# GpSimd makes the low part of every fourth weight unit of a float32 decoder layer

## The reference, cut to what matters

```
h = x + 1/2 * SwiGLU_1(norm(x))
z = norm(h) @ W_mix_in          # columns split into B, C, H (conv group), U, V (gMLP group)
h = h + concat(conv part, gated part) @ W_mix_out
h = h + XAttn(norm(h), norm(mem))
h = h + 1/2 * SwiGLU_2(norm(h))
out = norm_final(h)
```

## Time and profile before

| what | us |
|---|---|
| median of three runs | 2155.09 |
| lowest and highest run | 2153.47, 2155.34 |
| the profiled execution, its time | 2154.91 |
| its span, from the first to the last instruction | 2153.2 |
| PE busy | 2139.6 |
| DVE busy | 1388.9 |
| ACT busy | 991.8 |
| POOL busy | 2.3 |

### The profile page before, as it was taken

How to read it: one execution, slowest core, us unless ns; L and a number is a source line. 1 busy time by engine, 2 the same in 40 slices (tenths; PEclk the granted TensorE clock), 3 DMA queues, 4 the chain that set the end, 5 groups by cost and what they waited for, 6 DMA issues and landing times.

```text
span 2153.2 us, 25537 instructions
## 1 busy us (share of the span) xinstructions
PE 2139.6 (99%) x9584; PEld 1776.2 (82%) x9584; DVE 1388.9 (65%) x1611; ACT 991.8 (46%) x1104; POOL 2.3 (0%) x7
## 2 busy tenths in 40 slices
PE   9999999999999999999999999999999999999998
PEld 7888888888888888888888888888888888888886
DVE  5676667666475557868898554576676667764544
ACT  6444444444344444444554444454544444443433
POOL 0000000000000000000000000000000000000000
PEclk9999999999999999999999999999999999999999
DMA  7766666665556566665556555566666666665654
GB/s 232 219 186 199 192 193 193 195 195 191 193 181 206 181 201 184 199 216 184 185 191 201 165 163 174 162 216 195 191 191 195 194 193 188 196 196 194 195 194 139
DMA packets 159489, 412.20 MB, mean 191 GB/s; under 512 B 12604, under 2 KB 14260, under 8 KB 159028
## 3 DMA queue, kind: packets, MB, share of 16 engines
q1 hardware_dynamic: 158000, 410.04, 61.4%
q10 hardware_dynamic: 1412, 1.11, 0.2%
HBM read 409.01 MB, written 2.10 MB: 191 GB/s over the span
## 4 chain that ended last, share of the span: by engine, by line
PE 96%; DVE 2%; ACT 1%; DMA 0%; issue 0%; ACTq 0%; SPq 0%; DVEq 0%
PE ps L990 94%; PE ps L1019 1%; DVE w_lo L606 1%; PE ps L1003 1%; DVE ps L666 1%; PE ps L1068 0%; DVE convT L812 0%; DMA raw<-in_w_ffn_in 0%; ACT w_hi L336 0%; ACT convT L469 0%; PE ps L1134 0%; DVE stage L802 0%; ACTq L409 0%; ACT scratch L586 0%; ACT zT L466 0%
## 5 line engine op out<-in xcount | busy, mean ns | idle before, releaser
L606 DVE TENSOR_TENSOR w_lo<-raw,w_hi 128x1024 fp32r<-128x1024 f32 x768 | 936.2, 1224 | 707.5 <-ACT w_hi L336 700.9
L336 ACT ACTIVATE w_hi<-raw 128x1024 fp32r<-128x1024 f32 x767 | 810.7, 1061 | 1077.3 <-PE ps L990 1046.2
L990 PE MATMUL ps<-w_hi,xT_hi 128*128 128x512 f32 x1848 | 570.1, 390 | 1.6 <-DVE w_lo L606 1.6
L990 PE MATMUL ps<-w_lo,xT_hi 128*128 128x512 f32 x1848 | 569.2, 389 | 0.0
L990 PE MATMUL ps<-w_hi,xT_lo 128*128 128x512 f32 x1848 | 569.2, 389 | 0.0
L990 PEld LDWEIGHTS ps<-w_hi,xT_hi 128*128 128x128 f32 x1848 | 346.4, 188 | 73.8 <-DVE w_lo L606 1.2
L990 PEld LDWEIGHTS ps<-w_hi,xT_lo 128*128 128x128 f32 x1848 | 347.0, 188 | 72.0
L990 PEld LDWEIGHTS ps<-w_lo,xT_hi 128*128 128x128 f32 x1848 | 347.0, 188 | 72.0
L990 PE MATMUL ps<-w_hi,hidT_hi 128*128 128x512 f32 x704 | 218.3, 390 | 0.4 <-DVE w_lo L606 0.4
L990 PE MATMUL ps<-w_lo,hidT_hi 128*128 128x512 f32 x704 | 218.2, 389 | 0.0
L990 PE MATMUL ps<-w_hi,hidT_lo 128*128 128x512 f32 x704 | 218.2, 389 | 0.0
(11 more groups left out here) (126 smaller groups left out, 851.7 us busy)
## 6 DMA issues: line engine op xcount, KB each, us to landing
raw<-in_w_ffn_in SPq DMA_DIRECT2D x352, 512.0 KB, 4.2
raw<-in_w_ffn_out SPq DMA_DIRECT2D x176, 512.0 KB, 4.3
raw<-in_w_mix_in SPq DMA_DIRECT2D x80, 512.0 KB, 4.3
raw<-in_w_mix_out SPq DMA_DIRECT2D x32, 512.0 KB, 4.1
raw<-in_w_xq SPq DMA_DIRECT2D x32, 512.0 KB, 4.3
raw<-in_w_xk SPq DMA_DIRECT2D x32, 512.0 KB, 4.2
raw<-in_w_xv SPq DMA_DIRECT2D x32, 512.0 KB, 3.7
raw<-in_w_xo SPq DMA_DIRECT2D x32, 512.0 KB, 3.7
```

What stands on the lines that cost most here:

```text
L336: nc.scalar.activation(w_hi[:, k % RING, :], raw[:, k % RAW, :], ACT.Copy).then_inc(hi_ready, 1)
L606: nc.vector.tensor_tensor(w_lo[:, k % RING, :], raw[:, k % RAW, :], w_hi[:, k % RING, :].bitcast(F32), ALU.subtract).then_inc(lo_ready, 1)
L990: ins = nc.tensor.matmul(bank(s, t * GW + b * BLK, BLK), xs[:, k, t * P:(t + 1) * P], ws_[:, k % RING, b * BLK:(b + 1) * BLK], start=(k == ...
```

## The change

The low part of slot 3 goes to GpSimd, with a semaphore `lo_pool` of its own. DVE's `lo_units` leaves these units out. PE and SP wait for `lo_pool` or `lo_ready` according to the unit's slot. GpSimd makes the 66 units of the groups before `C`, then the mask of `w_spatial`, then the other 126.

```diff
+def low_parts(unit0, n):
+    base = (unit0.base if isinstance(unit0, Turn) else unit0) + n
+    pool = base % RING == 0
+    count = base // RING if pool else (RING - 1) * (base // RING) + base % RING
+    if isinstance(unit0, Turn):
+        count = unit0.i * (unit0.step // RING * (1 if pool else RING - 1)) + count
+    return pool, count
...
+        lo_pool = sem("lo_pool")
...
+        def wait_low(engine, unit0, n):
+
+            pool_made, count = low_parts(unit0, n)
+            engine.wait_ge(lo_pool if pool_made else lo_ready, count)
...
                     if not (isinstance(unit0, int) and unit0 + k < RAW):
-                        sp.wait_ge(lo_ready, unit0 + (k - RAW + 1))
+                        wait_low(sp, unit0, k - RAW + 1)
...
+            def low(hi_count):
+
+                pool.wait_ge(hi_ready, hi_count)
+                nc.gpsimd.tensor_tensor(w_lo[:, RING - 1, :], raw[:, RAW - 1, :], w_hi[:, RING - 1, :].bitcast(F32),
+                                        ALU.subtract).then_inc(lo_pool, 1)
+
+            units = sum(n for _, n in groups)
+            with pool.Fori(0, UNIT0["C"] // RING) as i:
+                low(i * RING + RING)
             pool.wait_ge(ws_loaded, 16)
             pool.affine_select(out=ws[:, :, :], in_=ws[:, :, :], compare_op=ALU.is_ge, fill=0.0, base=0,
                                pattern=[[0, HEADS], [-1, P]], channel_multiplier=1).then_inc(ws_masked, 1)
+            with pool.Fori(0, (units - UNIT0["C"]) // RING) as i:
+                low(i * RING + (UNIT0["C"] + RING))
...
             def lo_units(unit0, k0, k1):
                 for k in range(k0, k1):
+                    if k % RING == RING - 1:
+                        continue
                     dve.wait_ge(hi_ready, unit0 + (k + 1))
...
                 for k in range(k0, k1):
-                    pe.wait_ge(lo_ready, unit0 + (k + 1))
+                    wait_low(pe, unit0, k + 1)
```

More of the change, by code:

```diff
@@ L48, in starts, with __init__, __add__, __mul__ @@
     return at
+class Turn:
+    def __init__(self, i, base, step):
+        self.i, self.base, self.step = i, base, step
+    def __add__(self, n):
+        return self.i * self.step + (self.base + n)
+    def __mul__(self, n):
+        return self.i * (self.step * n) + self.base * n
+def low_parts(unit0, n):
[5 more added lines that the diff above has]
+    return pool, count
 def build(nc, x, mem, g_ffn1, w_ffn1_in, w_ffn1_out, g_mix, w_mix_in, conv_w, conv_b, g_gm_v, w_spatial, b_spatial,
@@ L271, in load_ffn_in @@
                     for j in range(2):
-                        load_units(ffn_in_src(w, i * GW + (1 + j) * BLK), i * (2 * KD) + (u0 + (1 + j) * KD), KD)
+                        load_units(ffn_in_src(w, i * GW + (1 + j) * BLK), Turn(i, u0 + (1 + j) * KD, 2 * KD), KD)
             def load_pair(name, w, n):
@@ L391, in ffn_in @@
                     for j in range(2):
-                        unit0 = i * (2 * KD) + (u0 + (1 + j) * KD)
+                        unit0 = Turn(i, u0 + (1 + j) * KD, 2 * KD)
                         hi_units(unit0, 0, 4)
-                        silu(j, unit0)
+                        silu(j, unit0 + 0)
                         hi_units(unit0, 4, 11)
```

## The result

| | before | changed |
|---|---|---|
| median of 20 runs, us | 2154.62 | 2157.38 |
| lowest and highest, us | 2152.9, 2155.41 | 2156.17, 2158.59 |
| span of the profiled execution, us | 2153.2 | 2156.2 |
| DVE busy, us | 1388.9 | 1172.5 |
| POOL busy, us | 2.3 | 469.1 |

The ratio is 1.0014, with a 95% interval from 1.0008 to 1.0021: 3.0 us slower (1.7 to 4.5), where 3.7 us was forecast.

What follows compares the result with a forecast made beforehand. TensorE was taken as the bound, with low parts nearly always early. The end 1.2, V 0.65 and U 1.9 us summed to 3.75 us, giving 2158.8 us (+0.17%) from a median of 2155.09, range 2154.8 to 2165.0.

Steps and rivals of the forecast that it cites:

- What bounds the kernel: Whole kernel: TensorE is the bound, busy 2139.6 of 2153.2 us; freeing DVE gains only where PE waits, 2.0 us in all.
- The price: GpSimd's subtraction in slot 3: 2.35 us plus 0.1 us to start, so its low part lands 1.18 us later than DVE's.
- my count by streams: Price of GpSimd's subtraction: three streams against the mask's two, 1.5 x 1.57 us, giving 2.35 us.
- my high end: Price of GpSimd's subtraction if all is done twice: 2 x 1.57 = 3.14 us.
- The two engines hold each other up: A DVE instruction with two SBUF inputs waits until GpSimd's has ended, and the other way round; one row showed 0.57 us.
- The end: Last unit, in slot 3: its low part comes 1.18 us later and counts in full, +1.2 us.
- Group U: Unit 6 of U: GpSimd's unit 7 and DVE's L835 run one after the other, so the low part is late, +1.9 us.
- The start of V: Convolution steps held until GpSimd's unit 15 ends, starting at 858.25 instead of 857.61; +0.65 us.
- ffn1_out1 and xo1: Transposing stretches: nothing, just; DVE held at unit 6 but in time, and unit 13 stays where it was.
- the slow rival: Subtraction near 3.14 us: end 2.0, V 1.45, U 2.7, ffn1_out1 and xo1 3.2 us; sum 9.4, 2164.5 us; chance 0.33.
- The quiet rhythm: Steady units: nothing lost; PE's margin goes from 5.58 to 4.40 us and the two engines hardly meet.
- the bound of 6.8 us: Quiet rhythm: PE would begin to wait only if the subtraction took 1.23 + 5.58 = 6.8 us.

Runs made afterwards that it cites:

- unit 7 of U alone: The kernel before, with the single low part of unit 7 of group U made by GpSimd and the other 767 by VectorE; 2155.59 us, ratio 1.0009.
- the copy: The changed kernel, with GpSimd copying the raw unit to the low part's place instead of subtracting (result altered); 2152.82 us, ratio 0.9993.
- its order changed: The changed kernel, with GpSimd starting unit 7 of U only once VectorE has made the low part of unit 6; 2155.13 us, ratio 1.0008.
- three units of B alone: The kernel before, with only units 3, 7 and 11 of group B made by GpSimd; 2153.78 us, ratio 0.9997.
- last low part in two halves: Changed kernel with units 15 of B, 7 of U and the last given back to VectorE, the last made in two halves; 2151.84 us, ratio 0.9992.
- twofold: The changed kernel, with GpSimd making each of its low parts twice over; 2196.78 us, ratio 1.0198.
- threefold: The changed kernel, with GpSimd making each of its low parts three times over; 2756.32 us, ratio 1.2795.

## Why the prediction came out as it did

The forecast was 2158.8 us, +0.17%; measured were 2157.38 us, +0.14%. The mechanism was right, and so were the two main places and their sizes. The price behind them came out by luck, the term for V was 0.4 us too large, and the nothing for ffn1_out1 and xo1 had a wrong reason. Step by step:

- **What bounds the kernel.** Right. DVE lost 216 us of busy time and TensorE gained nothing from it except at V, where one low part had been late.
- **The price, 2.35 us and 0.1 us to start.** 2.40 and 0.08 us (the high part at the end is over at 2135.63, GpSimd starts at 2135.71). This was luck. The mask's 1.57 us, from which I counted, held waiting already. In the kernel with unit 7 of U alone the same mask runs where no DVE instruction overlaps it:

```profile
55.05 1.09 POOL L379 TENSOR_SCALAR_AFFINE_SELECT ws<-ws 128x1024 f32<-128x1024 f32 x1 [53.51 <-DMA ws<-in_w_spatial]
```

So 0.48 us of 1.57 were waiting, behind the DVE subtraction of the earlier trace rows. From 1.09 us my count by streams gives 1.64 us and my high end 2.18 us, and the measured 2.40 us lies above both. Against one input (1.09 for the mask, 1.05 for the copy) the subtraction takes more than twice as long; these are other operations, so how much of it is the second input alone isn't shown.
- **The two engines hold each other up.** Right, and shown by the experiments with unit 7 of U alone and with its order changed. One row of 768 told it ahead, and the mask's own row was the other half: each of the two had been held by the other.
- **The end, +1.2 us.** TensorE's row moved by 1.18 us.
- **Group U, +1.9 us.** It moved by 1.84 us at unit 6 and 0.16 at unit 7.
- **The start of V, +0.65 us.** +0.25 us. The term was mis-sized: the convolution's first step took 2.62 us from 855.37, which less its own 0.48 makes 857.51, 0.2 us before GpSimd's recorded end at 857.71, and the relief had brought all of this forward by a little more than the 0.65 us that I took: ACT begins to empty H 1.09 us earlier than in the earlier trace rows, of which 0.3 us are the shift from the start.
- **ffn1_out1 and xo1: nothing.** The number was right and the reason wrong. I had DVE held at unit 6 and the margin at unit 13 staying at 0.07 us. The rows:

```profile
612.41 2.36 DVE L687 SCALAR_TENSOR_TENSOR h<-ps,h 128x1024 f32<-128x1024 f32 x2 [0.34 <-PE ps L1031]
...
623.33 1.20 DVE L647 TENSOR_TENSOR w_lo<-raw,w_hi 128x1024 fp32r<-128x1024 f32 x1
624.56 2.93 DVE L707 STREAM_TRANSPOSE ps<-h 32x512 f32<-32x512 f32 x4
...
624.49 2.40 POOL L355 TENSOR_TENSOR w_lo<-raw,w_hi 128x1024 fp32r<-128x1024 f32 x1 [8.47 <-ACT w_hi L375]
```

The low part of unit 3 used to stand in DVE's queue ahead of the residual step and waited there for its high part. With it gone, the residual step starts as soon as TensorE is done with the old group, and all of the stretch is over two microseconds earlier (the low part of 6 at 623.33, where the earlier trace rows has 625.87). GpSimd's unit 7 then falls on transposes, which it doesn't hold. The smallest margin in the group is 3.75 us now. So the slow rival's 3.2 us in these stretches would not have come about either; its sum was too high by that much. The kernel with each low part made twice bears this out: at a price of 4.9 us TensorE's rows don't move by more than 0.11 us at any of the first 19 units of ffn1_out1 nor anywhere in xo1.

- **The quiet rhythm.** Nothing was lost, as said, but the bound of 6.8 us left out a loop. The turn of the `raw` slot, high part, low part and load, fills TensorE's 10.9 us at 10.9 - 1.06 - 4.3 - 0.1 = 5.4 us, an estimate from the rows. At 4.9 us the load already released the high part of slot 3 in 89 of 191 turns, without a wait of TensorE in the quiet rhythm; at 7.4 us in 108. The measured 603 us rule out the 115 us that my bound gave for 7.4 us, but that price lies above both bounds, so where between 4.9 and 7.4 us the rhythm breaks isn't shown.

What stays open: the two clusters of runs, and with them the shift of -0.3 us at the start. The landing of the first loads doesn't separate the clusters: the second weight unit's high part begins at 8.76 us in the kernel with three units of B alone and at 9.62 us before, both in the upper cluster, and at 9.66 us (last low part in two halves) and 10.11 us (unit 7 of U after unit 6) in the lower. What separates them, in all ten profiles but those of the twofold and threefold kernels, is the length of TensorE's first weight products. Before, upper cluster, and then the kernel with the last low part in two halves, lower cluster:

```profile
9.17 1.91 PE L1068 MATMUL ps<-w_hi,xT_lo 128*128 128x512 f32 x4
...
8.74 1.09 PE L1135 MATMUL ps<-w_hi,xT_lo 128*128 128x512 f32 x4
```

In the five profiles of the upper cluster the first eight products all take 0.63 us or more, in the five of the lower they come down to 0.4 us by the fourth at the latest. 0.63 us is also the length of a product at a granted clock of 0.50 in the twofold experiment, so a clock that rises later would fit. It isn't shown: the profile gives the granted clock as 1.00 from the start in both.

## What to carry to other kernels

Before work is moved to an idle engine, ask two things. First, whether anyone waits for the engine that is relieved: here 235 us of relief were worth 0.8 us, and three of 192 instructions brought all of it. Second, what the helper's instruction will run beside: here a GpSimd instruction that reads SBUF held a VectorE instruction with two SBUF inputs nearly to its own end (2.12 us of 2.40), so it should fall on transposes, on steps that read PSUM, or on idle time, and never just ahead of a long two-input step on the path. In an in-order queue, a step that is taken out also frees what stood behind its wait, which can be worth more than its duration (over 2 us for 1.2 us in ffn1_out1). A measured duration that is taken as a base for a price should be one without such company: the mask's 1.57 us were 1.09 us alone. And a wait that grows long can cost TensorE its clock on top, 14.5 of 43 us in the twofold experiment.

## What the runs showed of the hardware

- GpSimd: 2.40 us for a 128x1024 float32 subtraction with two inputs from SBUF, 1.05 us for a copy and 1.09 us for the mask of the same size, both with one input. DVE: 1.23 us for the subtraction.
- The hold goes both ways and lasts nearly to the end of the instruction that came first. DVE's L876 was held 2.12 us, a convolution step took 2.62 instead of 0.48 us, and GpSimd took 3.31 and 3.85 us in place of 2.40. A GpSimd duration in the profile thus contains its own standing still. One place doesn't follow the order of the recorded starts: at 1147.96 us of the changed kernel GpSimd's row begins 0.16 us ahead of DVE's subtraction, yet DVE's takes 1.20 us and GpSimd's 3.63 us, and the same in five of the experiments.
- Steps of DVE with at most one tile in SBUF, the rest in PSUM, or with one input, were not held. Beside GpSimd's subtraction the transposes of 32x256 kept a median of 457 ns (some 110 of them that overlap it by more than half; 456 ns for the others), and the gating step, PSUM times one SBUF tile with a scalar per partition, 750 ns (34; 742 ns). Before the change nothing had shown this.
- The Trainium skill, SBUF — State Buffer, section Who interferes with whom, says this of the port pair that DVE and GpSimd share: an exclusive lock, taken by whoever starts first; outside its two-port modes, DVE contends for it only with two SBUF inputs, and only with a GpSimd instruction that reads SBUF. The runs agree with the numbers above, but for the one place at 1147.96 us.
- TensorE's clock: at the granted clock of 0.50 behind a wait of 7.29 us, a pair of products took 1.05 us instead of 0.62.
